# Key scores of a PEER search formed head by head beside the query projection, and a search that starts there

## The reference

```python
def peer_ffn(x, wq, subkeys, u, v):
    q = (x @ wq).reshape(b, s, PEER_HEADS, 2, PEER_QUERY_DIM // 2)      # 8 heads, 2 halves of 64
    sc = jnp.einsum('bshtd,htkd->bshtk', q, subkeys)                    # 128 keys per half
    top_s, top_i = lax.top_k(sc, PEER_TOPK)                             # 16 of 128
    cand = top_s[..., 0, :, None] + top_s[..., 1, None, :]              # 16 x 16 sums
    best_s, best_c = lax.top_k(cand.reshape(..., 256), PEER_TOPK)
    i1 = take_along_axis(top_i[..., 0, :], best_c // PEER_TOPK)
    i2 = take_along_axis(top_i[..., 1, :], best_c % PEER_TOPK)
    idx = i1 * PEER_KEYS + i2                                           # 128 experts of 16384 a token
    gate = softmax(best_s)
    hid = einsum('td,tkd->tk', x, u[idx]);  act = gelu(hid) * gate
    return einsum('tk,tkd->td', act, v[idx])
```

## Time and profile before

| | |
|---|---|
| median of 3 runs | 3421.98 us (3418.57 to 3427.04) |
| span of the profiled execution | 3423.6 us |
| TensorE busy, share of the span | 3337.5 us, 97% |
| VectorE | 2792.0 us, 82% |
| ScalarE | 1919.5 us, 56% |
| GpSimd | 458.3 us, 13% |
| granted TensorE clock, mean | 0.990 |
| memory traffic | 968.98 MB, 283 GB/s |

### The profile page before, as it was taken

One profiled execution on the slowest core, in us unless ns is written; L12 is line 12 of the kernel. 1 busy time (PEld: TensorE's weight loads), 2 busy tenths in 40 slices (PEclk: granted clock), 3 DMA queues, 4 the chain that ended last, 5 costly groups with the idle time before them and its releaser, 6 DMA issues.

```text
span 3423.6 us, 51716 instructions
## 1 busy us (share of the span) xinstructions
PE 3337.5 (97%) x19476; PEld 3003.1 (88%) x19476; DVE 2792.0 (82%) x3859; ACT 1919.5 (56%) x3354; POOL 458.3 (13%) x264
## 2 busy tenths in 40 slices
PE   8999999999999999999998999999999999999998
PEld 7888779999999988888887877999999998888887
DVE  4664657999999978889986745899999988888897
ACT  4555445545666655555555545554566665555555
POOL 0000000011222212123300000001122221222230
PEclk9999999999999999999999989999999999999999
DMA  6543245689899989999984334568899998999995
GB/s 253 184 173 135 93 154 197 216 299 329 332 361 361 361 319 357 360 358 378 378 307 153 112 130 159 197 220 320 299 364 361 361 348 334 356 358 366 380 380 218
DMA packets 169069, 968.98 MB, mean 283 GB/s; under 512 B 18896, under 2 KB 52688, under 8 KB 55376
## 3 DMA queue, kind: packets, MB, share of 16 engines
q1 hardware_dynamic: 132048, 698.61, 54.7%
q0 software_dynamic: 36864, 268.45, 20.9%
HBM read 951.26 MB, written 15.73 MB: 282 GB/s over the span
## 4 chain that ended last, share of the span: by engine, by line
PE 80%; DVE 16%; DMA 1%; ACT 1%; issue 1%; DVEq 0%; ACTq 0%
PE ps L889 79%; DVE wl L1478 7%; DVE arena L1643 2%; DMA raw<-in_u 1%; ACT wh L520 0%; DVE arena L1695 0%; DVE arena L1705 0%; PE ps L1076 0%; DVE arena L1685 0%; DVE arena L1701 0%; DVE xx L1496 0%; DMA arena<-in_v,idx 0%; DVE arena L1680 0%; DVE arena L1679 0%; DVE arena L1663 0%
## 5 line engine op out<-in xcount | busy, mean ns | idle before, releaser
L1478 DVE TENSOR_TENSOR wl<-raw,wh 128x1024 fp32r<-128x1024 f32 x1264 | 1525.7, 1219 | 493.4 <-ACT wh L520 490.8
L889 PE MATMUL ps<-xx,wh 128*128 128x384 f32 (+1 forms) x5504 | 1713.4, 373 | 36.0 <-DVE wl L1478 29.4
L520 ACT ACTIVATE wh<-raw 128x1024 fp32r<-128x1024 f32 x1264 | 1333.7, 1057 | 619.8 <-PE ps L889 532.1
L889 PE MATMUL ps<-xx,wl 128*128 128x192 f32 (+1 forms) x5504 | 1423.5, 259 | 0.0
L889 PE MATMUL ps<-wh,act 128*128 128x512 f32 x3584 | 1190.5, 390 | 4.1 <-DVE act L1501 4.0
L889 PEld LDWEIGHTS ps<-xx,wh 128*128 128x128 f32 x5504 | 1036.0, 188 | 103.2 <-DVE wl L1478 36.6
L889 PEld LDWEIGHTS ps<-xx,wl 128*128 128x128 f32 x5504 | 1051.2, 191 | 0.5
L889 PE MATMUL ps<-wl,act 128*128 128x512 f32 x2304 | 897.1, 389 | 0.0
L889 PEld LDWEIGHTS ps<-wh,act 128*128 128x128 f32 x3584 | 673.6, 188 | 146.7 <-DVE act L1501 3.5
L889 PEld LDWEIGHTS ps<-wl,act 128*128 128x128 f32 x2304 | 433.0, 188 | 89.5
L1449 POOL DMA_INDIRECT arena<-in_v,idx x128 | 261.7, 2045 | 837.8 <-DVE arena L1816 818.1
(11 more groups left out here) (212 smaller groups left out, 1720.8 us busy)
## 6 DMA issues: line engine op xcount, KB each, us to landing
raw<-in_u SPq DMA_DIRECT2D x256, 1024.0 KB, 6.4
raw<-in_v SPq DMA_DIRECT2D x256, 1024.0 KB, 7.4
raw<-in_w SPq DMA_DIRECT2D x119, 1024.0 KB, 4.8
h_scratch<-hring SPq DMA_DIRECT2D x128, 96.0 KB, 5.6
hring<-h_scratch SPq DMA_DIRECT2D x128, 96.0 KB, 7.4
arena<-in_memT SPq DMA_DIRECT2D x4, 512.0 KB, 6.5
arena<-in_xT SPq DMA_DIRECT2D x4, 512.0 KB, 7.7
arena<-in_urows,idx POOLq DMA_INDIRECT x128
```

The costliest lines, as they stand in the source:

```text
L520: nc.scalar.activation(wh[:, j, :], raw_piece(p), ACT.Copy).then_inc(hi_ready, 1)
L889: return nc.tensor.matmul(out, lhs, rhs, start=start, stop=stop, **kw)
L1478: v.tensor_tensor(wl[:, j, :], raw_piece(p), wh[:, j, :].bitcast(F32), ALU.subtract).then_inc(lo_ready, 1)
```

## The change

The score products of head h stand after query slab h + 1 on TensorE, those of head 7 after the first expert slab. ScalarE copies each head's scores out (`scores_out`), where VectorE did it in groups of four units. SyncE loads the subkeys after the third query slab instead of before the first expert slab, behind a wait for x. The query slabs are written out, no longer a loop, and the first expert slab follows without a break: the last query slab is folded in its middle. VectorE's `experts` takes over the low halves from query piece 3 on: five at once, and then the units, each of the first eight waiting for its head's scores. `UNIT_LOWS` gives the first three units 4, 4 and 5 low halves, the next seven 6, unit 10 thirteen and units 11 to 15 twelve; unit 10 has its dots in gaps 4 and 6, unit 15 in gaps 2 and 4. The index is replicated before trip 5 instead of trip 7.

```diff
-REP_TRIP = 7
+REP_TRIP = 5
-UNIT_LOWS = [(1, 1, 1, 1, 1, 1, 0)] * PEER_H + [(1, 1, 1, 1, 1, 1, 1), (1, 2, 1, 2, 1, 1, 1)] * (PEER_H // 2 - 2) + [(1, 1, 1, 1, 1, 2, 1), (1, 2, 1, 2, 1, 2, 1)] * 2
-UNIT_DOTS = [(0,) * 7] * (PEER_H + 2) + [(0, 0, 0, 0, 0, 0, 1)] + [(0, 0, 1, 0, 1, 0, 1)] * 5
+WQ_LOWS = 5
+UNIT_LOWS = ([(1, 0, 1, 0, 1, 1, 0)] * 2 + [(1, 1, 1, 0, 1, 1, 0)] + [(1, 1, 1, 1, 1, 1, 0)] * 7
+             + [(2, 2, 2, 2, 2, 2, 1)] + [(2, 2, 2, 2, 2, 1, 1)] * 5)
+UNIT_DOTS = ([(0,) * 7] * (PEER_H + 2) + [(0, 0, 0, 0, 1, 0, 1)] + [(0, 0, 1, 0, 1, 0, 1)] * 4
+             + [(0, 0, 1, 0, 1, 0, 0)])
...
+        def queries(layer, row, p0):
+            stream(row, p0, RAW_SLABS)
+            sp.wait_ge(x_ready, QX * (3 if layer == 0 else 5))
+            sp.dma_start(subk[:, :, :], dram["subk"][layer, :, :, :]).then_inc(subk_in, 16)
+            sp.dma_start(rep, dram["rep"]).then_inc(subk_in, 16)
+            stream(row + RAW_SLABS, p0 + 2 * RAW_SLABS, S_WQ - RAW_SLABS)
...
+        def scores_out(layer, h):
+            act.wait_ge(sc_ready, PEER_H * layer + h + 1)
+            b = 2 + 2 * (h % 3)
+            nc.scalar.activation(sc.rearrange("p (t h) w k -> p t h w k", t=NT)[:, :, h],
+                                 ps[:, b:b + 2, 0:TOK].rearrange("p w (t k) -> p t w k", t=NT),
+                                 ACT.Copy).then_inc(sc_evac, 1)
+        def queries(layer, p0, t0):
+            def between(k):
+                if k:
+                    scores_out(layer, k - 1)
+            t_stage(p0, t0, S_WQ, copy_out(lambda k: qt[:, k, :]), done=AHEAD, between=between, through=True)
...
+        def scores(layer, h, t0):
+            if h == 0:
+                pe.wait_ge(subk_in, 32 * (layer + 1))
+            pe.wait_ge(evac_done, t0 + h + 1)
+            if h >= 3:
+                pe.wait_ge(sc_evac, PEER_H * layer + h - 2)
+            for t in range(NT):
+                for half in range(2):
+                    rows = slice(64 * half, 64 * half + 64)
+                    last = mm(ps[:, 2 + 2 * (h % 3) + half, t * P:(t + 1) * P],
+                              qt[rows, h, t * P:(t + 1) * P], subk[rows, h, :], True, True)
+            last.then_inc(sc_ready, 1)
...
-            for b in range(UNITS // 4):
-                dve.wait_ge(sc_ready, 4 * layer + b + 1)
-                bank = 2 + 2 * (b % 3)
-                v.tensor_copy(sc[:, 4 * b:4 * b + 4, :, :].rearrange("p u t k -> p t u k"),
-                              ps[:, bank:bank + 2, :].rearrange("p t (u k) -> p t u k", u=4)).then_inc(sc_evac, 1)
-                low(1)
-            dve.wait_ge(sc_evac, 4 * layer + 4)
+            low(WQ_LOWS)
...
                 if head:
+                    if i < PEER_H:
+                        dve.wait_ge(sc_evac, PEER_H * layer + i + 1)
                     own.mark(v.tensor_copy(s0, sc[:, i, :, :]))
```

More of the change, by code:

```diff
@@ L520, in hi, with t_stage @@
             nc.scalar.activation(wh[:, j, :], raw_piece(p), ACT.Copy).then_inc(hi_ready, 1)
-        def t_stage(p0, t0, n, evac, done=0, beside=None, last=None):
+        def t_stage(p0, t0, n, evac, done=0, beside=None, last=None, between=None, through=False):
             def close(k, bank, *pieces):
@@ L528, in close @@
                     hi(q, j)
+                if between is not None:
+                    between(k)
                 if last is not None and k == n - 1:
@@ L541, in t_stage @@
                 q = 2 * k + RING
-                close(k, k % 2, *((p0 + q + e, (q + e) % RING) for e in range(2) if k < n - 2))
+                close(k, k % 2, *((p0 + q + e, (q + e) % RING) for e in range(2) if through or k < n - 2))
                 if beside is not None:
@@ L675, in trip @@
                         softmax_exp()
+                    if first and s == 0:
+                        continue
                     ahead = [] if final and s == slabs - 1 else [2 * s + 2, 2 * s + 3]
[L677 to L680, removed]
+                    take_side(u0, i * slabs + (s - 1), (s - 1) % 2, ND)
                     for n in ahead[:-1]:
                         hi(i * (2 * slabs) + (u0 + n), n % RING)
-                    if not (first and s == 0):
-                        gelu(i * slabs + (s - 1), s - 1)
+                    if first and s == 1:
+                        scores_out(layer, PEER_H - 1)
+                    gelu(i * slabs + (s - 1), s - 1)
                     for n in ahead[-1:]:
@@ L895, in fold, with slab_t @@
                 .then_inc(fold_done, 1)
-        def slab_t(piece, slab, par_, s4, first=False, x_from=None, then=None, lone=False, t0=0):
+        def slab_t(piece, slab, par_, s4, first=False, x_from=None, then=None, lone=False, t0=0, side_t0=None):
             if not first:
@@ L917, in slab_t @@
                 if e == 0 and not lone:
-                    fold(slab - 1, 1 - par_, t0)
+                    fold(slab - 1, 1 - par_, t0 if side_t0 is None else side_t0)
                 if then is not None:
@@ L1139, in outs, with queries, then @@
             last.then_inc(o_ready, 1)
-        def experts(layer, u0, v0, t0):
-            pe.wait_ge(subk_in, 32 * (layer + 1))
-            pe.wait_ge(evac_done, t0)
-            for b in range(UNITS // 4):
[L1146 to L1155, removed]
+        def scores(layer, h, t0):
[10 more added lines that the diff above has]
+            last.then_inc(sc_ready, 1)
+        def queries(layer, p0, t0, x_count):
+            for k in range(S_WQ):
+                def then(e, k=k):
+                    if e and k:
+                        scores(layer, k - 1, t0)
+                slab_t(p0 + 2 * k, t0 + k, k % 2, k, x_from=QX * (x_count - 1) if k == 0 else None, then=then,
+                       lone=k == 0)
+        def experts(layer, u0, v0, t0):
             def spread(q):
@@ L1171, in trip, with then @@
                     then = None
+                    if first and s == 0:
+                        def then(e):
+                            if e:
+                                scores(layer, PEER_H - 1, t0 - S_WQ)
                     if spreads:
@@ L1176, in trip @@
                     slab_t(i * (2 * slabs) + (u0 + 2 * s), i * slabs + (t0 + s), s % 2, s, then=then,
-                           lone=first and s == 0, t0=NS)
+                           t0=NS, side_t0=0 if first and s == 0 else None)
             def replicate(values):
@@ L1182, in experts @@
             trip(0, BODY, first=True)
-            pe.wait_ge(sc_evac, 4 * (layer + 1))
+            pe.wait_ge(sc_evac, PEER_H * (layer + 1))
             for b in range(4):
@@ L1775, in experts @@
                         dot()
-            assert next(at_piece) == 2 * S_EXP and next(at_dot) == PAIRS
+            assert next(at_piece) == 2 * (S_WQ + S_EXP) and next(at_dot) == PAIRS
             dve.wait_ge(slot_free, PAIRS * (2 * layer + 1))
@@ L1978, in _ @@
         norm(0, P_WQ0, P_WQ0)
-        split_t(P_WQ0, S_WQ, done=AHEAD)
-        experts(0, P_U0, P_V0, S_OUT)
+        experts(0, P_WQ0, P_V0, S_OUT)
         norm(1, P_INB, P_INB)
```

29 lines of the change are left out of this document (13 added, 16 removed).

## The result

The changed kernel takes 3415.24 us (median of 7 runs, 3407.49 to 3420.08), the kernel before 3422.15 us beside it (3418.57 to 3427.04). The ratio is 0.9968 with a 95% interval of 0.9958 to 0.9979: 11 us, 7 to 14, where 14.7 were forecast. A second measurement on another occasion gave 0.9961 [0.9947, 0.9974]. It is faster, clear of the noise, by about the 0.3% that such a measurement can tell. The two medians stand only 6.9 us apart; against the 3411.7 us that the forecast had called faster, the median falls short and the ratio just reaches it. The median lies 8 us above the 3407 forecast, outside the forecast's own range of 3401 to 3413 and inside 3390 to 3418. One run among all that follow, of the kernel with pairs and dots moved, took 4293.79 us at a mean granted clock of 0.696, and the ratios leave it out.

A forecast was written before the change was run, and what follows sets the result against it. TensorE held 80% of the chain, waiting at places for VectorE (16%). Gains of 7.1 us in layer 0 and 7.6 in layer 1 took the 3423.6 us span to 3408.9, a 3407 us median; range 3390 to 3418, own 3401 to 3413.

The forecast's parts named there:

- The stalls that stay: TensorE still waits for low halves, mainly where units 11 to 14 end: 9.2 us a layer instead of 15.1 and 15.6.
- six lone dots: Single dots between low halves, six a layer: each takes 4.35 us over one 2.35 us piece, 0.1 beyond cover, 0.6 together.
- the cover: How late VectorE may be with a piece before TensorE stalls, since ring buffers must be free: 1.9 us, however idle before.
- The replicate: TensorE's wait for the expert index goes, with one piece, 2.35 us, of room gained: gain 1.4 us a layer.
- VectorE's time: Units 11 to 15: too much work before, 2.6 us a piece against 2.35; after, 27.4 us against 28.2 a unit.
- idle some tenths a unit: Sign expected in the new profile: VectorE idle some tenths of a us per unit in units 11 to 15.
- The score products: Eight blocks in the slabs at 0.63 us a head (bounds 0.48, 0.87), 5.0 against 3.84; net loss 0.2 a layer.
- the switch: Cost of TensorE changing tiling mode around each head's block of score products: 0.15 us a block.
- ScalarE and DMA: Eight score copies of 0.60 us between high halves, and the subkey and fourth query slab loads waiting for x: all free.
- all waits go: Rival: VectorE's units fit, 27.4 against 28.2 us, so no low-half waits remain; gain 33 us, 3389 us; chance 0.15.
- Stalls as large as before: Rival: cover at each dot 0.9 us shorter, stalls grow 6 us a layer, gain 2 to 3, 3418 us; chance 0.14.
- The slower case: Rival: raw slabs arrive late beside gathers, 0.91 us each, up to 14.6 us a layer; 3436 us; chance 0.07.

The follow-up runs named there:

- the kernel with pairs and dots moved: Changed kernel with score products of two heads in one block and the search's dots in gaps 0, 2 and 4; 3396.82 us, ratio 0.9918.
- the edits that cure the new stalls: Here on the kernel before: odd high half made before the activation function, dots in gaps 0, 2 and 4; 3425.24 us (one run).
- the two edits: Changed kernel with dots in gaps 0, 2 and 4 and the odd high half made before the activation function; 3393.99 us (one run).

## Why the prediction held, and where it was off

- **The stalls that stay.** Forecast per layer: four of 1.95 us, one of 0.75, 0.6 at six lone dots, 9.2 in all. Measured: 9.4 and 9.3. Each of the four stretches from gap 4 to the seam lost 0.1 to 0.2 us at its first dot and 1.7 at the seam, 1.9 together; unit 10 lost 0.6; the six lone dots lost nearly 0.2 each, some 1.1 in all; 0.2 stands at the replicate. The place, the count and the mechanism were right, and experiments removed the stalls from either side, by the dots' place and by the cover. Only the lone dots were mis-sized: two numbers of over 4 us are subtracted there, and what is left, 0.1 us, is as small as the error of the cover of 1.9 us. That the sum came within 0.2 us is luck in part, since some 0.5 too much at the lone dots stands against 0.4 too little at the seams.
- **The replicate.** The idle 1.4 us went, and the slab around it, 1.9 us over the cadence, now has 0.2 over. Waits of both kinds together gave 7.7 and 8.1 us less, forecast 7.3 and 7.8.
- **VectorE's time.** That it was short of time before was right: the edits that cure the new stalls leave the old ones, and VectorE is busy without a gap there. The sign "idle some tenths a unit" was wrong: after the change it waits 2.7 us for high halves in a unit of 30.3 us. The forecast's own terms give that, 28.2 + 1.95 - 27.4 = 2.8.
- **The score products: the term that was mis-sized.** Forecast 0.63 us a head, measured 0.87, as much as the upper bound. The step that failed is the switch, put at 0.15 us and measured at 0.37 to 0.41, and the cause is a misread row. The timeline merges neighbours of one line and names the shape of the first alone, so the eight records of the earlier trace rows are not all of 192 columns:

```profile
L889 PE MATMUL ps<-arena x8: 269/297/428, 1901.9 to 1902.4; 64*128 64x192 f32 x4, 64*128 64x128 f32 x4
```

At the block's rate these take 0.60 us and not 0.72, which leaves 0.27 of 0.87. The rest is in the distances beside the block: 0.20 us ahead of it where 0.11 is usual, and 0.34 behind the next product where 0.23 is usual in these slabs. With them the row costs 0.09 + 0.74 + 0.11 = 0.94, and the switch 0.34, close to what the experiments gave. That the upper bound of 0.87 equals the measured figure is chance. So the query part, first query fold to the second expert slab's fold, grew from 54.1 to 55.5 us: a loss of 1.4 a layer instead of 0.2. The Trainium skill, TensorEngine Tiling (Array Packing), Key Properties, says that a change of tiling mode drains TensorE; the runs agree in kind, with 0.41 us there and back.

- **The sum.** 7.7 + 8.1 - 1.4 - 1.4 = 13.0 against 14.7. The score products and what stands around them cost 2.4 more than forecast, and 0.7 came back from the waits.
- **ScalarE and DMA.** ScalarE's copies cost nothing that shows: 0.59 us each between high halves, and in the kernel before, moving them to ScalarE changed nothing. No wait for `in_u` stands among the waits from 480 to 862 us. One query slab a layer, by its place the fourth, which now waits for x, came late: ScalarE waited 0.6 and 0.9 us for it, and TensorE did not wait.
- **The rivals.** That all waits go was not this kernel, but it was near: the two edits brought it about. Stalls as large as before did not come, because they were of another kind. The slower case did not show, and TensorE waited for no low half in the query slabs.

What the forecast lacked was a question: why must the odd high half follow the fold? I read the order of the earlier trace rows as given, though nothing but ScalarE's program order tied the two. That was worth 6.3 us a layer here.

## What to carry over

Idle time of an engine does not prove that its neighbour cannot starve. Here VectorE works in order and may run only a few pieces ahead, and TensorE stalled wherever a single stretch between two hand-overs went beyond that cover. So count two things apart, the work per round and the longest stretch against the cover, and cure the one that binds; each edit is worth little while the other binds. Before a price is taken from a merged row, ask for the shapes in it. To lengthen the cover, look at what stands in front of the instruction that starts it, and at what that in turn waits for.

## What the runs showed of the hardware

**A fixed price of 64-row products among 128-row ones.** 0.37 to 0.41 us for a block there and back, beside 0.46 for four fp32 products of 128 columns (eight records).

**A clock that differs between runs of one program.** From 330 to 400 us, in the stage ahead of the query slabs, the granted clock was 1.00 in the first profile of the changed kernel and 0.83 in the second; over all fourteen profiles it lay between those, and the first query fold between 490.5 and 498.6 us, later the lower the clock: 0.98 went with 491.9 to 492.0, 0.88 with 496.0 to 497.8. Here the windows of the first profile, then of the second:

```profile
330.00:340.00 10.00, 7.86 (x63) 6.21 (x63) 3.21 (x7) 6.43 (x20) 0.00 (x0) 1.00 0.02 7
...
370.00:380.00 10.00, 8.05 (x58) 7.07 (x58) 8.67 (x14) 3.31 (x5) 0.00 (x0) 1.00 0.01 2
```

```profile
330.00:340.00 10.00, 7.85 (x47) 5.99 (x45) 2.18 (x4) 5.48 (x15) 0.00 (x0) 0.77 0.05 20
...
370.00:380.00 10.00, 6.20 (x13) 4.03 (x14) 7.16 (x9) 3.56 (x6) 0.00 (x0) 0.50 0.00 0
```

TensorE is busy without a gap from 310 to 330 us in both runs and alike from 330 to 340, and the clock falls in one run and not in the other; from 370 to 380 us it is there at 0.50, its lower level of 1.2 GHz. The first query fold comes 8 us later for it, more than a layer's gain and about as much as the two spans differ (7.6). The seven runs of the changed kernel agree: their times rise from 3407.49 to 3420.08 us as their mean granted clock falls from 0.992 to 0.989. What decides it the profiles don't show. A change of this size is better read from a stage's length than from the span.
